# Whole-height fp32r products with zeroed halves, weight panels rounded in place, projections scaled in PSUM

## What is computed

```
h = rmsnorm(x); proj = h @ w_in                      # 1024 x 4888
o_nsa = compressed, selected and sliding-window attention, 8 heads, 2 key groups
        score = q . k * scale + bias (+ a mask of the 4 selected 64-key blocks)
o_sb  = stick-breaking attention, 8 heads, head size 64
        a = exp(log_sigmoid(z) + sum of log_keep of the later keys), z = q . k * scale
x = x + (sig(g0) * (o_nsa @ w_up_nsa) + sig(g1) * (o_sb @ w_up_sb)) @ w_out
x = x + square(relu(rmsnorm(x) @ w_ff1)) @ w_ff2
out = rmsnorm(x)
```

## Time and profile before

| | |
|---|---|
| time, median of 3 runs | 885.01 us (884.01 to 885.42) |
| the profiled execution | 883.92 us, of it span 882.1 us |
| mean granted TensorE clock | 0.991 |
| TensorE busy | 856.1 us (97%) |
| VectorE, ScalarE, GpSimd busy | 463.4, 331.6, 285.8 us |

### The profile page before, as it was taken

One profiled execution on the slowest core, in us unless ns is written; L12 is line 12 of the kernel. 1 busy time (PEld: TensorE's weight loads), 2 busy tenths in 40 slices (PEclk: granted clock), 3 DMA queues, 4 the chain that ended last, 5 costly groups with the idle time before them and its releaser, 6 DMA issues.

```text
span 882.1 us, 11354 instructions
## 1 busy us (share of the span) xinstructions
PE 856.1 (97%) x4012; PEld 661.9 (75%) x4012; DVE 463.4 (53%) x767; ACT 331.6 (38%) x579; POOL 285.8 (32%) x123
## 2 busy tenths in 40 slices
PE   5999999899999999999999999999999999999996
PEld 3778988676666555656888878888888888888895
DVE  4444467754545545453176668877117612761254
ACT  5323223466664445455533433333113311331221
POOL 4243343311112111111444444444444444444430
PEclk9999999899999999999999999999999999999998
DMA  9652221200015000003322222222222222222202
GB/s 320 266 144 67 82 88 62 96 25 0 1 34 182 25 24 5 23 23 114 124 94 99 96 96 95 96 96 95 95 95 95 95 95 95 95 95 95 96 1 96
DMA packets 25045, 77.60 MB, mean 88 GB/s; under 512 B 3662, under 2 KB 6918, under 8 KB 24623
## 3 DMA queue, kind: packets, MB, share of 16 engines
q1 hardware_dynamic: 23756, 75.77, 25.7%
q10 hardware_dynamic: 1251, 1.32, 0.6%
HBM read 73.90 MB, written 2.13 MB: 86 GB/s over the span
## 4 chain that ended last, share of the span: by engine, by line
PE 89%; DVE 5%; ACT 2%; DMA 2%; issue 1%; SPq 1%; DVEq 0%; ACTq 0%
PE bank L1121 60%; PE bank L1356 4%; PE bank L1101 3%; PE bank L1103 3%; PE bank L1102 3%; PE bank L1278 3%; PE bank L1320 2%; PE bank L1289 2%; PE bank L1338 2%; PE bank L1261 1%; PE bank L1319 1%; DMA wraw<-in_panels 1%; DMA xs<-in_xT 1%; PE bank L1185 1%; DVE sk L819 1%
## 5 line engine op out<-in xcount | busy, mean ns | idle before, releaser
L447 POOL TENSOR_TENSOR wlo<-wraw,whi 128x1024 fp32r<-128x1024 f32 x117 | 282.7, 2419 | 562.3 <-ACT whi L478 301.3
L1121 PE MATMUL bank<-hh,wlo 128*128 128x512 f32 x320 | 131.9, 412 | 10.7 <-DVE hl L742 10.7
L1121 PE MATMUL bank<-hh,whi 128*128 128x512 f32 x320 | 129.2, 404 | 0.0
L1121 PE MATMUL bank<-hl,whi 128*128 128x512 f32 x320 | 128.6, 402 | 0.0
L478 ACT ACTIVATE whi<-wraw 128x1024 fp32r<-128x1024 f32 x63 | 66.0, 1056 | 120.3 <-PE bank L1121 77.7
L1121 PE MATMUL bank<-r_h,wlo 128*128 (+2 forms) x288 | 105.4, 366 | 0.0
L1121 PE MATMUL bank<-r_l,whi 128*128 (+2 forms) x288 | 105.2, 365 | 0.0
L1121 PE MATMUL bank<-r_h,whi 128*128 (+2 forms) x288 | 105.2, 365 | 0.0
L1121 PE MATMUL bank<-h2h,wlo 128*128 128x512 f32 x256 | 100.1, 391 | 0.1
L1121 PE MATMUL bank<-h2h,whi 128*128 128x512 f32 x256 | 99.6, 389 | 0.0
L1121 PE MATMUL bank<-h2l,whi 128*128 128x512 f32 x256 | 99.6, 389 | 0.0
(11 more groups left out here) (218 smaller groups left out, 1354.1 us busy)
## 6 DMA issues: line engine op xcount, KB each, us to landing
wraw<-in_panels SPq DMA_DIRECT2D x117, 512.0 KB, 3.3
xs<-in_xT SPq DMA_DIRECT2D x8, 256.0 KB, 7.3
w1k<-in_w SPq DMA_DIRECT2D x1, 2048.0 KB, 9.7
w1v<-in_w SPq DMA_DIRECT2D x1, 2048.0 KB, 14.2
hank<-bias_by_distance SPq DMA_DIRECT2D x4, 512.0 KB, 6.2
x_res<-in_xT SPq DMA_DIRECT2D x1, 2048.0 KB, 7.8
out_dram<-x_res SPq DMA_DIRECT2D x16, 128.0 KB, 1.8
cstb<-in_cst SPq DMA_DIRECT2D x1, 640.0 KB, 13.5
```

The source lines that it names most:

```text
L447: nc.gpsimd.tensor_tensor(wlo[:, s], wraw[s][:], whi[:, s].bitcast(F32), ALU.subtract).then_inc(w_lo, 1)
L1121: ins = M(b[:, cols], lhs, (xl if a == 1 else xh)[:, row + k, cols], start=(m == 0), stop=(m == 23))
```

## The change

Five edits. (1) The operands that lay on 64 or 16 rows are laid out on 128, the other rows zeroed once (`kn_l`, `sq_lo`, `maskT`), and the bf16 masks become fp32r; so every product in `logits` and `scores` is of 128 rows. (2) `wraw` now shares its memory with `wlo`: GpSimd subtracts in place, and the next load into the slot waits for `w_used`, counted when TensorE has finished the last product with the low half (product 22 of the 24). (3) `evac` scales in the bank and keeps it; ScalarE rounds out of the bank, VectorE subtracts out of it, and only then it is free. (4) In the sparse part the splits stand four iterations later and begin with an earlier panel number. (5) The residual is loaded in four pieces between panels.

```
-        wraw = [place(f"wraw{i}", [P, 8, P]) for i in range(RING)]
         whi = place("whi", [P, RING, 8, P], F32R)
+        at_wlo = top[0]
         wlo = place("wlo", [P, RING, 8, P], F32R)
+        wraw = [place(f"wraw{i}", [P, 8, P], at=at_wlo + 4096 * i) for i in range(RING)]
...
-                    sp.wait_ge(w_lo, p - RING + 1 + RING * i)
+                    sp.wait_ge(w_used, p - RING + 1 + RING * i)
...
-            panel_loop(P_GM + GM_SB + 5, P_UP + 3)
+            panel_loop(P_GM + GM_SB + 4, P_UP)
             sparse_pv_done(sp, 4 * PAIRS - 1)
-            sp.dma_start(x_res[:], xT).then_inc(xres_in, 16)
-            panel_loop(P_UP + 3, NPANEL)
+            panel_loop(P_UP, P_UP + RING)
+            for n in range(RING):
+                sp.dma_start(x_res[:, 2 * n:2 * n + 2], xT[:, 2 * n:2 * n + 2, :]).then_inc(xres_in, 16)
+                panel(P_UP + RING + n)
+            panel_loop(P_UP + 2 * RING, NPANEL)
...
             def round_tmp(p, *parts):
-                stored(act, ("pan", p))
+                act.wait_ge(t_in, nt[0] + 1)
+                b = bank[USE[("pan", p)][0]]
                 for a, dst in parts:
-                    ins = A(dst, tmp[a, nt[0] % 2], ACT.Copy)
+                    ins = A(dst, b[a, :], ACT.Copy)
...
-                if i == 0:
-                    split(P_GM + GM_SB + RING)
-                if i % 10 in (5, 7) and i < UNITS:
-                    split_half(P_GM + GM_SB + 1 + i // 10 + RING, i % 10 // 7)
+                if i >= 9 and i % 10 in (9, 1) and i < UNITS:
+                    split_half(P_GM + GM_SB + RING + (i - 9) // 10, i % 10 % 9)
...
+            for g in range(G):
+                V.memset(kn_l[g][GROUP[1 - g]].bitcast(F32), 0.0).then_inc(zero_done, 1)
+            V.memset(sq_lo[1][GROUP[0]].bitcast(F32), 0.0).then_inc(zero_done, 1)
+            V.memset(maskT[:].bitcast(F32), 0.0).then_inc(zero_done, 1)
...
-                ins = V.scalar_tensor_tensor(out=tmp[:, i % 2], in0=ps[:], scalar=scale, in1=rstd_b[:],
-                                             op0=ALU.mult, op1=ALU.mult)
-                emptied(ins, name)
+                V.scalar_tensor_tensor(out=ps[:], in0=ps[:], scalar=scale, in1=rstd_b[:],
+                                       op0=ALU.mult, op1=ALU.mult).then_inc(t_in, 1)
+                dve.wait_ge(t_in, i + 1)
                 dve.wait_ge(t_hi, i + 1)
                 for a, lo, hi in parts:
-                    ins = V.tensor_tensor(lo, tmp[a, i % 2], hi.bitcast(F32), ALU.subtract)
-                ins.then_inc(t_lo, 1)
+                    ins = V.tensor_tensor(lo, ps[a, :], hi.bitcast(F32), ALU.subtract)
+                emptied(ins, name)
...
+                    if m == 21 and p < NPANEL - 4:
+                        ins.then_inc(w_used, 1)
...
                     M(o, keys[:, p, kk], queries[:, P * k:T], start=(k != 3), stop=False, skip_group_check=True)
-                    M(o, keys[a, p, kk], sq_l[a, p, P * k:T], start=False, stop=False, skip_group_check=True)
-                    ins = M(o[:, 0:P], ident_bf[:], diag_bf[:], start=False, stop=False, skip_group_check=True)
+                    M(o, keys[:, p, kk], sq_lo[odd][:, p, P * k:T], start=False, stop=False, skip_group_check=True)
+                    ins = M(o[:, 0:P], ident_r[:], diag_r[:], start=False, stop=False, skip_group_check=True)
...
-                ins = M(b[:, 0:n], qn[g][a, p, P * r:P * r + P], kn_l[a, br, 0:n], start=False, stop=not masked)
+                ins = M(b[:, 0:n], qn[g][:, p, P * r:P * r + P], kn_l[g][:, br, 0:n], start=False, stop=not masked)
...
-                    ins = M(b[:, 0:n], maskT[:, r - 2, :], blk_bf[:, g, 0:n], start=False, stop=True)
+                    ins = M(b[:, 0:n], maskT[:, r - 2, :], blk_r[:, g, 0:n], start=False, stop=True)
```

More of the change, by code:

```diff
@@ L205, in block_kernel @@
         kn_h = place("kn_h", [P, 2, T], F32R)
-        kn_l = place("kn_l", [P, 2, T], F32R)
+        kn_l = [place(f"kn_l{g}", [P, 2, T], F32R) for g in range(G)]
         at_sbq = top[0]
@@ L227, in block_kernel @@
         negones = place("negones", [P, P], F32R)
-        ident_bf = place("ident_bf", [P, P], BF16)
-        diag_bf = place("diag_bf", [P, P], BF16)
-        blk_bf = place("blk_bf", [2 * NB, G, T], BF16)
+        ident_r = place("ident_r", [P, P], F32R)
+        diag_r = place("diag_r", [P, P], F32R)
+        blk_r = place("blk_r", [P, G, T], F32R)
         rcol = place("rcol", [P, RT])
@@ L235, in block_kernel @@
         vc = place("vc", [P, G, DH])
-        maskT = place("maskT", [2 * NB, 2, P], BF16)
+        maskT = place("maskT", [P, 2, P], F32R)
         nmin = place("nmin", [P, 4])
@@ L241, in block_kernel @@
         pct = place("pct", [P, G, T])
+        sq_lo = [sq_l, place("sq_l_odd", [P, PAIRS, T], F32R)]
         ckv = place("ckv", [P, 2, T], at=at_pct)
@@ L592, in _ @@
                 if i == 3:
-                    act.wait_ge(t_lo, 6 + 1)
+                    stored(act, ("pan", P_SQK))
                     queries_twice(0)
@@ L665, in _ @@
                 if i == 0:
+                    split(P_GM + GM_IN_ATT - 2 + RING)
                     split(P_GM + GM_IN_ATT - 1 + RING)
@@ L934, in _ @@
                 else:
-                    evac(("pan", P_SQK + i), DH ** -0.5, (ALL, sq_l[:, p], sq_h[:, p]))
+                    evac(("pan", P_SQK + i), DH ** -0.5, *((GROUP[o], sq_lo[o][GROUP[o], p], sq_h[GROUP[o], p]) for o in range(2)))
                 if i == 1:
@@ L1138, in value_panels @@
                             o = b[:, 2 * P * a:2 * P * a + 2 * P]
-                            ins = three(o, lh, ll, whi[:, s:s + 2, k, :], wlo[:, s:s + 2, k, :], k == 0, k == KT - 1)
+                            low = M(o, lh, wlo[:, s:s + 2, k, :], start=(k == 0), stop=False)
+                            mid = M(o, ll, whi[:, s:s + 2, k, :], start=False, stop=False)
+                            ins = M(o, lh, whi[:, s:s + 2, k, :], start=False, stop=(k == KT - 1))
+                    if i == 1:
+                        low.then_inc(w_used, 1)
+                        mid.then_inc(w_used, 1)
                     filled(ins, name)
@@ L1209, in cmp_scores @@
                 pe_.wait_ge(kc_split, 2)
-                pe_.wait_ge(t_lo, 6)
+                stored(pe_, ("pan", P_QN + 3))
                 b = claim(pe_, ("cs", r))
@@ L1248, in logits @@
                 p, odd = divmod(h, 2)
-                a, keys = GROUP[odd], sk[odd]
+                keys = sk[odd]
                 queries = sq_odd[p % 2][:] if odd else sq_h[:, p]
@@ L1296, in _ @@
             pe_.wait_ge(cast_done, 5)
+            pe_.wait_ge(zero_done, 5)
             stored(pe_, ("sv", 2))
@@ L1388, in _ @@
                         for k in range(PAIRS):
-                            ins = three(b[:], whi[:, s, 4 * m + k, :], wlo[:, s, 4 * m + k, :], oh[:, k, :], ol[:, k, :], k == 0, k == PAIRS - 1)
+                            low = M(b[:], wlo[:, s, 4 * m + k, :], oh[:, k, :], start=(k == 0), stop=False)
+                            M(b[:], whi[:, s, 4 * m + k, :], ol[:, k, :], start=False, stop=False)
+                            ins = M(b[:], whi[:, s, 4 * m + k, :], oh[:, k, :], start=False, stop=(k == PAIRS - 1))
+                        if m == 1:
+                            low.then_inc(w_used, 1)
                         filled(ins, name)
```

30 lines of the change are left out of this document (15 added, 15 removed).

## The result

The changed kernel takes 871.69 us (median of 4 runs, 870.26 to 873.22) against 885.21 us for the kernel before on the same chip (884.01 to 885.57). The ratio is 0.984, 95% interval 0.982 to 0.987: faster by 1.6%. The forecast was 859 us, its range 849 to 870. So the sign is right, the time lies above the range, and of the 25.8 us expected 13.7 came (span 868.4 us instead of 882.1).

What follows compares the result with a forecast made beforehand. TensorE, busy 97% of the span, was taken as the bound. Terms -24 (sparse part), -9 (logits), +2.5 (projections), +2 (up to out) and +2.7 (out to MLP) sum to -25.8 us, from 885.01 to 859 us, range 849 to 870.

Steps and rivals of the forecast that it cites:

- Edit 1, the sparse part: Sparse-part products: equal heights remove gaps of some 0.19 us per height change, saving 30.8 us gross, 24 us net.
- The give-back: Sparse-part turns: 24 come some 0.3 us late, waiting for ScalarE's copy behind exponential and half panel; 7 us lost.
- Rival C: Sparse part: VectorE and ScalarE become the bound, every turn waits, give-back 15 to 20 us; 870 us, chance 10%.
- Edit 1, the logits: Logits: a head takes 1.69 us instead of 2.84 with one height; saves 9 us, bounds 7 to 11.
- get dearer: Logits masks: the bf16 mask was followed after 0.04 us, an fp32r mask takes 0.11.
- Rival B: Products: gaps belong to changes of operand or bank, not height, so edit 1 gives nothing; 894 us, chance 2%.
- Edit 2, projections: Projections to last transpose: late splits add 1.8 and 1.5 us, less 1.1 for faster subtractions; +2.5 us, bounds 0 and 6.
- Up to out and out to MLP: Last mixed tile's rounding and the square before the MLP wait for late splits; +2 us and +2.7 us.
- The clock: Behind the idle time at the last transposes the fall to half speed repeats; no new fall is expected.
- rival D: Clock: without the fall 3.5 us lower, 855 us; with new falls at two new waits 7 higher, 866 us; inside A's 82%.
- Edits 4 and 5: Sparse-part splits and the residual's quarter loads: cost nothing, since panels are rounded early and queues have empty time.
- The zeroing: Opening: some 4.5 us of zeroing lies in VectorE's idle time before its first subtraction; 1 to 2 us if uncovered.

Runs made afterwards that it cites:

- gate_between: Against both_first_slots, the last gate product of each sparse-part iteration stands behind the turn instead of ahead of it; 853.3 us.
- copy_first: Against the changed kernel, ScalarE's copy of the turned weights stands ahead of the exponential in each sparse-part iteration; 868.26 us.
- both_first_slots: The changed kernel with round_first and copy_first together, and ScalarE's twelve sparse-part half panels moved to iterations where TensorE makes value products; 849.87 us.
- both_first_bf16: The changed kernel with round_first and copy_first together, and the masks bf16 again but on 128 rows; 851.95 us.
- half_height: The changed kernel with edit 1 taken back: low products on 64 rows, masks bf16 on 16 rows; 899.79 us.
- round_first: Against the changed kernel, ScalarE's roundings, GELU and squares in projections, up and out stand ahead of the split that stood before them; 857.12 us.
- all_three: both_first_slots with the masks bf16 on 128 rows as in both_first_bf16; 851.04 us.
- ring_alone: The kernel before with edits 2, 4 and 5 only, without scaling in PSUM and without whole height; 902.23 us.

## Why the prediction came out as it did

Of the 25.8 us forecast 12.1 did not come. Over half of them, 6.6, is the gross saving of edit 1 in the sparse part; 2.1 and 1.1 are the late splits in the projections and around the out projection, 1.3 the clock at the MLP's start.

**Edit 1, the sparse part: right mechanism, gross saving too large.** The prediction said that "the four products of the earlier trace rows are alike" afterwards and take 0.92 us, 30.8 us in all. They take 1.01, and the sum over 64 units is some 24.2 us (the distances of single units, kind by kind, add up to 24.7). The step that failed is reading each excess in the earlier trace rows as a change of height of "some 0.19 us". Of the 0.41 behind L1319 only half is that: in a logits block of the kernel before, where no transpose stands ahead, the change from 128 to 64 rows costs 0.09. Its timeline, between the first two rows:

```profile
210.04 0.49 PE L1261 MATMUL bank<-sq_l,sk 64*128 64x512 f32 x1
```

That is 0.32 us behind the product of 209.72, against 0.23 among equals. The other 0.09 belong to the transposes ahead and stay, as gate_between shows. At some 0.09 for each of 64 units that is 6 us, nearly the whole error of this term.

**The give-back: right cause, the size in part by luck.** Forecast 7 us. Gross 24.2 less the 16.7 measured leaves 7.5. copy_first and both_first_slots took 3.5 and 1.2 us of it away for 48 units, an estimated 6.3 for 64 (stage 5: 158.0 to 151.6), so its cause was shown to be what the prediction said: the copy behind exponential and half panel. The size was put together from 24 turns 0.3 us late, and the trace has a few long waits instead, five in 48 units, up to 1.44 us. What the prediction did not list is that VectorE's order stands next behind it. Rival C gave the right order of time (870 us) for the wrong reason: the give-back stayed at 7, it is the saving that was smaller.

**Edit 1, the logits: right**, 8 x (2.84 - 1.77) = 8.6 us against 9. Its remark that masks "get dearer" from 0.04 to 0.11 was wrong without consequence: a bf16 mask and the product behind it take 0.04 and 0.26 us in both_first_bf16, an fp32r one and its follower 0.06 and 0.22 to 0.23. The rest of the 9.5 us of stage 4 is, by estimate, 1.9 from the shorter stretch at half clock less 1.3 for longer waits (0.82 for a gate tile at 182.18, 1.03 instead of 0.55 for the last values).

**Rival B, out.** half_height settles it. The rule of the Trainium skill, "TensorE: Matmul & The Clock Gate", Part 3, by which loads overlap running products only when the row group differs, is contradicted by this case: loads of whole height are pulled ahead of a running product of whole height by 0.23 us. The Trainium skill, "TensorE: Matmul & The Clock Gate", Part 2, also allows a pull-ahead into a background weight buffer, and with that the rows agree.

**Edit 2, projections: mis-sized.** Forecast +2.5 (bounds 0 and 6; its own terms, +1.8, +1.5 and -1.1, add up to 2.2), measured +4.6: 1.6 at `hidT`, as the 1.5 forecast, and 3.0 behind it where at most 1.0 was left after "1.1 for faster subtractions". The named waits of TensorE there are 6.8 us instead of 4.2. Two things were not in the sum. The wait ahead of the earlier compressed transposes, at 137 us, went from 0.26 to 2.13. And GpSimd's subtraction moved with the split to another place in VectorE's chain: L906 took 1.41 us under it at 166.75, where it takes 0.17 in round_first. In the kernel before it lay on another step of the same chain, which takes 0.42 us in the changed kernel:

```profile
159.90 1.29 DVE L885 TENSOR_TENSOR c_p<-c_p,c_m 128x248 f32<-128x248 f32 x1
```

So the move itself costs only some 0.4 us. The Trainium skill, "SBUF — State Buffer", section "SBUF: two separate sides", states a lock by which a VectorE operation on two SBUF tiles and a GpSimd operation that reads SBUF exclude each other. The traces agree with it (1.41 us under GpSimd's subtraction, 0.17 without), but that it was the lock and nothing else was not tried apart.

**Up to out and out to MLP: a little low.** Forecast 2 + 2.7, measured 5.8 in stage 7. The first wait is 2.39 us and costs 2.6 with the slower start behind it. At the second TensorE stands 3.35 us from start to start (507.92 to 511.27) where it stood 0.53 before, 2.8 more. The rest, 0.3 us, are the three products behind it, 1.10 us where they took 0.80, in part at the lower clock, which the sum had not. round_first takes 6.2 us off the stage, all of it and 0.4 more than before the change.

**The clock: half right.** "I expect the fall to repeat and no new one": the fall repeated, shorter, and of the two new waits one, at the MLP's start, had a new one behind it, 1.3 us instead of the 3.5 per fall in rival D.

**Edits 4 and 5: right.** No panel in the sparse part is late, and stage 6 did not move by 0.1 us.

**The opening, not foreseen.** The start of the first weight pair varies between traces by more than the 0.9 us that it adds here (see below), so this part of the profiled difference is not ascribed to the change. The zeroing stayed covered, as forecast: VectorE's first subtraction starts at 5.88 us, before at 5.98.

The account: -25.8, +6.6 for the gross saving and +0.7 for the give-back and its rounding, -0.5 logits with clock, +2.1 projections, +1.1 out and up, +1.3 clock in the MLP, +0.9 opening: -13.6 against -13.7 measured.

**What stays open.** Why the stretch at half clock behind the last transposes was shorter after a longer wait than before, and why the clock falls behind a wait of some 2 us in one execution (half_height at 493.30, idle 2.26; round_first at 175.02, idle 2.24) and not in another (the changed kernel at 464.50, idle 2.39; all_three at 176.46, idle 2.20). In round_first and its successors, the wait of 2.24 us for L961; nothing was tried on it.

## What to carry to other kernels

An excess distance between two products has to be split by its two neighbours before it is promised as a saving: look for the same pair somewhere else in the trace with another predecessor. An edit that makes a step wait longer (here `split` for its load) is paid for by whatever stands behind that step in its engine's queue; moving the small steps of ScalarE's program ahead of it gave back more than the whole of its price, and the kernel with the lowest time here, both_first_slots at 849.87 us, is 2.3% below the changed one by its ratio. Compare traces by stages between landmarks, not by absolute times, or the variation of the opening is read as an effect.

## What the runs showed of the hardware

- Weight loads: a change of row height between neighbouring products of 512 columns costs 0.09 to 0.10 us from 128 to 64 rows and some 0.19 from 64 to 16 (the 16-row one bf16). Back to 128 rows the cost is spread over two distances: 0.42 to 0.43 and 0.34 us instead of 0.23 twice behind 64 rows (some 0.3 in all), 0.32 and 0.34 behind 16 rows (some 0.2), in the kernel before and in half_height alike. Equal heights cost nothing, and zeroed rows are free. The first fp32r product behind fp32 transposes has its follower 0.09 us late.
- An fp32r mask product on 128 rows costs the same as a bf16 one. The product behind a bf16 one is recorded 0.04 us after it, and the one behind that so much later that the two distances add up to those of fp32r products.
- The clock: behind idle times of 2.2 to 2.4 us it was at half for some 3 us in some executions and not at all in others (the cases stand under what stays open), so such a wait costs its own length and sometimes 1.5 us more.
- The opening differs by 5 us between these traces, of kernels whose opening is nearly the same. In three of them (ring_alone, both_first_slots, both_first_bf16) the granted clock between 7 and 27 us reads 1.00, and the first weight pair began at 22.8 to 23.5 us; in the other eight it was 0.83 to 0.91, and it began at 25.7 to 27.9. Seven runs of the kernel before in one job took 880.84 to 887.19 us, the longer ones at the lower mean clock (0.993 falling to 0.988); no trace shows where in them the time lies. A single run tells nothing below 0.7%.
